# An eighth unit of hgrn's input weights kept in SBUF between two tiles, by way of an idle router place and a copy on ScalarE

## The chip, the cores and the metric

The kernel runs on one core of a Trainium2 chip, in one launch. The metric is the device time of the launch in microseconds. The kernel before takes 1483.97 us in the median of three runs (1483.34 to 1484.56).

## What is computed

A trunk of two layers over 256 positions of 1024 values, all in float32. Layer 0 mixes positions with windowed attention, layer 1 with HGRN2, a gated linear recurrence. After each comes PEER, a mixture of 16384 single-neuron experts. Cut to what matters:

```python
def hgrn2(xn, w_in, lower_bound, out_gain, w_out):
    q, f, i, g = split(xn @ w_in, 4)            # w_in is 1024 x 4096: 16 MiB
    ...                                          # gates, chunkwise recurrence
    return (rmsnorm(o, out_gain) * silu(g)) @ w_out

def block(xb):                                   # peer_ffn, 128 positions at a time
    q = xb @ w_q                                 # the router: 8 heads, 2 halves
    ...                                          # top 16 of 16384 for each head and position
    u = u_tab[expert]
    act = gelu(einsum('pd,phkd->phk', xb, u))
    return einsum('phk,phkd->pd', gates * act, v_tab[expert])

for i in range(2):
    h = h + (swa_attention, hgrn2)[i](rmsnorm(h, mixer_norm[i]), ...)
    h = h + peer_ffn(rmsnorm(h, ffn_norm[i]), ...)
```

## The kernel before, in words

The 256 positions are two tiles of 128, so the PEER blocks are four **phases** (layer 0 tile 0, layer 0 tile 1, layer 1 tile 0, layer 1 tile 1) of 128 **rows**. A row is one gather on POOL: for each of 128 positions the u and v rows of one expert, 8 KB, one MiB in all, into one of eight places of `ring`. DVE takes the dot product with xn (L1135), ScalarE Gelu, coefficient and a diagonal matrix of it (`diag`, L572), and PE adds the v rows into PSUM by that diagonal (L1545), or, for the rows of `VECTOR_ROWS`, DVE adds them into h (L1144). Gather n waits until the place of row n - 8 is free (`slots_free` from PE, `v_added` from DVE).

Beside the rows of phase p the engines do the mixer and the router for the other tile: attention in phase 0, hgrn for tile 0 in phase 1, hgrn for tile 1 in phase 2. Every engine has the same program: `foreground` of the row, then `beside(p, q)`, which says what belongs to row q. hgrn takes two heads at a time (four steps i of 20 rows, from row 8). Step i does `project` in 14 rows, levels of the chunk scan (`scores` on PE, `produce` and `extend` on DVE) in rows r = 16 to 24, the output in r = 26 (`h_o`), squares of it on ScalarE in r = 27, and the projection out in r = 33 to 36. The scan's scratch is in the first 2048 words of `mix` (hkq, sufpre, kq). The fourth step of phase 1 is done with it at row 94; phase 2 writes it next at row 22.

hgrn's input weights come in 32 **units** of one MiB, 16 for each tile; unit x is quarter x % 4 of the weights of step x // 4. Tile 1 takes the heads in the order 3, 2, 0, 1, so that it begins with the weights with which tile 0 ended. A unit lies in a **place**: 0 to 2 are in `wmix`, 3 and 4 in the room of router pair 3 (`wroute`), 5 and 6 in that of router pair 2. `UNIT_KEPT` says which units of tile 1 are still there from tile 0 (16 to 22), `UNIT_PLACE` where each lies, and `UNIT_LOADS` before which row SP's program has its load. SP's program is in order and has no clock of its own: what it issues is held by waits alone. A load into place 0 to 2 waits until the last unit there has been used (`h_proj`), one into a router place until the router has been used for phase 1 (`r_score`).

The four router pairs of layer 1 are loaded by `load_route` (L463 on): pair 0 in phase 1, pair 1 at row 104 of phase 1, which in order is right behind the third output load `load_hgrn_out` (row 85), pairs 3 and 2 in phase 2 when the kept units in their room have been used. PE asks for pair 1 at row 120 of phase 1, for the third unit of phase 2's router (`pair_projects`, `route_begin`).

Functions that the change and the prediction's steps touch: `unit_weights` (L382), `load_unit` (L444), `load_route` (L463), `copy` (L571, its operation L572), ScalarE's `beside` (L697), `project` (L1396) and the tables at L140.

Of the kernel before, what the change touches and what calls it, by code (L numbers as in the profile page):

```python
# [16 lines left out]
D = 1024  # L17
KT = D // P
EPS = 1e-6
HALF = 512  # L20
ITERS = 4
# [27 lines left out]
MIXED = 105  # L49
UNITS = 5  # L50
UNIT_HOMES = 3
UNIT_PLACES = 7
PAIR_ORDER = ((0, 1, 2, 3), (0, 1, 2, 3), (0, 1, 3, 2), (0, 1, 3, 2))
CHUNKS = 6
FIRST_CHUNK = (0, 2, 3, 4, 5)
HEAD_EXP = (115, 124)
RESIDUAL = 32


# [76 lines left out]
def unit_part(x):  # L136
    return x % 4 // 2, x % 2


UNIT_PLACE = (0, 1, 2, 0, 1, 2, 0, 1, 5, 6, 2, 0, 3, 4, 1, 0,  # L140
              3, 4, 1, 0, 5, 6, 2, 1, 0, 2, 1, 0, 2, 1, 0, 2)
UNIT_KEPT = {16: 12, 17: 13, 18: 14, 19: 15, 20: 8, 21: 9, 22: 10}
UNIT_LOADS = {0: {40: 0, 61: 1, 82: 2},
              1: {12: 3, 15: 4, 19: 5, 22: 6, 32: 7, 33: 8, 34: 9, 35: 10, 39: 11, 59: 12, 60: 13, 62: 14, 63: 15},
              2: {19: 23, 22: 24, 39: 25, 42: 26, 52: 27, 56: 28, 59: 29, 62: 30, 72: 31}}


def unit_load(x):
# [20 lines left out]
def trunk(nc, x, cos, sin, masks_attn, masks_hgrn, ident_in, place_in, gains, mixer_gain, sinks, lb_raw, out_gain,  # L169
          attn_in, attn_out, hgrn_in, hgrn_out, route_w, experts, out):  # L170
    with ExitStack() as ctx:
# [192 lines left out]
        h_decayed, h_decayedT_ps, h_decayedT = sem("h_decayed"), sem("h_decayedT_ps"), sem("h_decayedT")  # L364
        h_o, h_sq, h_ims, h_rstd = sem("h_o"), sem("h_sq"), sem("h_ims"), sem("h_rstd")
        h_on_ready, h_oT_ps, h_oT_ready = sem("h_on_ready"), sem("h_oT_ps"), sem("h_oT_ready")
        h_outproj = sem("h_outproj")
        r_proj, r_qT, r_score, r_top = sem("r_proj"), sem("r_qT"), sem("r_score"), sem("r_top")
        r_done, r_gate, g_shift, g_exp = sem("r_done"), sem("r_gate"), sem("g_shift"), sem("g_exp")

# [11 lines left out]
        def unit_weights(place):  # L382
            if place < UNIT_HOMES:
                return wmix[:, place]
            pair, at_ = ITERS - 1 - (place - UNIT_HOMES) // 2, (place - UNIT_HOMES) % 2
            return wroute[:, pair, at_ * 2 * D:(at_ + 1) * 2 * D]

# [54 lines left out]
        @block.sync  # L442
        def _(sp):
            def load_unit(x):  # L444
                place, (j, half) = UNIT_PLACE[x], unit_part(x)
                tile, i = x // 16, x // 4 % ITERS
                if x < UNIT_HOMES:
                    sp.wait_ge(a_outproj, ITERS + 1 + x)
                elif place < UNIT_HOMES:
                    sp.wait_ge(h_proj, last_use_of_place(x) + 1)  # L450
                else:
                    sp.wait_ge(r_score, CHUNKS + (6 if place < UNIT_HOMES + 2 else 5))
                sp.dma_start(unit_weights(place), hgrn_in[heads_at(tile, i) * 2 + j][:, half * 2 * D:(half + 1) * 2 * D]).then_inc(whgrn_in[place], 16)

            def load_hgrn_out(tile, i):
                n = tile * ITERS + i
                if n > 0:
                    sp.wait_ge(h_outproj, n)
                else:
                    sp.wait_ge(a_outproj, 2 * ITERS)  # L460
                sp.dma_start(bands(wmix[:, UNIT_HOMES], HH), hgrn_out[heads_at(tile, i)]).then_inc(whgrn_out_in, 16)

            def load_route(layer, pair):  # L463
                if layer and pair < 2:
                    sp.wait_ge(r_score, CHUNKS + 3 + pair)
                elif layer:
                    sp.wait_ge(h_proj, 18 if pair == 3 else 22)
                elif pair == ITERS - 1:
                    sp.wait_ge(a_outproj, ITERS)
                elif pair == 2:  # L470
                    sp.wait_ge(a_proj, 2 * ITERS)
                sp.dma_start(wroute[:, pair], route_w[layer * ITERS + pair]).then_inc(wroute_in[pair], 16)

            def hgrn_loads(p, q):
                tile = 1 - own_tile(p)
                for i in range(ITERS):
                    r = q - HEAD - HGRN_PERIOD * i
                    if r == 37 and i < ITERS - 1:
                        load_hgrn_out(tile, i + 1)

            sp.dma_start(h[:, 0], x[0]).then_inc(x0_in, 16)
            for to, of in ROPE:
                sp.dma_start(to, of).then_inc(rope_in, 16)
            half = AIN // 2
            sp.dma_start(win0(0)[:, 0:half], attn_in[0][:, 0:half]).then_inc(wattn0_in[0], 16)
            sp.dma_start(win0(0)[:, half:AIN], attn_in[0][:, half:AIN]).then_inc(wattn0_rest, 16)
            sp.wait_ge(x0_in, 16)
            sp.dma_start(win0(1), attn_in[1]).then_inc(wattn0_in[1], 16)
            sp.wait_ge(wattn0_rest, 16)
            sp.dma_start(win0(2), attn_in[2]).then_inc(wattn0_in[2], 16)  # L490
            sp.wait_ge(wattn0_in[1], 16)
            sp.dma_start(win0(3), attn_in[3]).then_inc(wattn0_in[3], 16)
            sp.dma_start(h[:, 1], x[1]).then_inc(x1_in, 16)
            sp.wait_ge(wattn0_in[2], 16)
            for g in range(ITERS):
                sp.dma_start(wout0(g), attn_out[g]).then_inc(wout0_in[g], 16)
            load_route(0, 0)
            sp.dma_start(gain_rows[:], gains).then_inc(gain_in, 16)
            for to, of in LATE:
                sp.dma_start(to, of).then_inc(late_in, 16)  # L500
            load_route(0, 1)
            load_route(0, 3)
            for p in range(PHASES):
                for q in range(PER):
                    if p == 0 and q == LAST_AHEAD[-1] + 1:
                        load_route(0, 2)
                    elif p == 1 and q == 4:
                        load_route(1, 0)
                    elif p == 1 and q == 104:
                        load_route(1, 1)  # L510
                    elif p == 2 and q == 15:
                        load_route(1, 3)
                    elif p == 2 and q == 36:
                        load_route(1, 2)
                    if q in UNIT_LOADS.get(p, {}):
                        load_unit(UNIT_LOADS[p][q])
                    if p == 0:
                        if q == 103:
                            load_hgrn_out(0, 0)
                    elif p < 3:  # L520
                        hgrn_loads(p, q)
                    if p == 3 and q == 5:
                        sp.wait_ge(norm_done, norm_at(3, 0) + 1)
                        sp.dma_start(out[0], xn[:, 0]).then_inc(out_done, 16)
            sp.wait_ge(norm_done, norm_at(3, 1) + 1)
            sp.dma_start(out[1][:, HALF:D], xn[:, 1, HALF:D]).then_inc(out_done, 16)
            sp.wait_ge(out_done, 16 * (TILES + 1))
# [40 lines left out]
        def _(act):  # L568
# [128 lines left out]
            def beside(p, q):  # L697
# [27 lines left out]
                for i in range(ITERS):  # L725
                    if p == 0:
                        attention(i, q - ATTN_HEAD - ATTN_PERIOD * i)
                    else:
                        hgrn(tile, i, q - HEAD - HGRN_PERIOD * i)
                if q == MIXED + 2:  # L730
                    act.wait_ge(h_ready, evacuations(p) + 1)
                    norm_squares(norm_at(p, 1), tile)
                elif q == MIXED + 5:
                    norm_sqrt(norm_at(p, 1), rroute[:, tile:tile + 1])
# [530 lines left out]
        def _(pe):  # L1265
# [130 lines left out]
            def project(n, r):  # L1396
# [6 lines left out]
                for u in range(2):  # L1403
                    x = 4 * n + r // 7 * 2 + u
                    load, half = unit_load(x), unit_part(x)[1]
                    place = UNIT_PLACE[x]
                    w = unit_weights(place).rearrange("p (k c) -> p k c", k=KT // 2)
                    for c in range(3):
                        for k in range(KT // 2):
                            step, cost = cost * 7 // 32, cost + 1 + c // 2  # L1410
                            if step != r % 7:
                                continue
                            if c == 0 and k == 0:
                                pe.wait_ge(whgrn_in[place], 16 * loads_into_place(load))
                            first, end, key = u == 0 and k == 0 and c == 0, u == 1 and k == KT // 2 - 1, half * KT // 2 + k
                            if c < 2:
                                last = nc.tensor.matmul(ab[:, j, c * P:(c + 1) * P], w[:, k, c * P:(c + 1) * P], xTs[:, 0, key],  # L1417
                                                        start=first, stop=end, skip_group_check=True)
                            else:
                                last = nc.tensor.matmul(ab[:, j, 2 * P:4 * P], xTs[:, 0, key], w[:, k, 2 * P:4 * P],  # L1420
                                                        start=first, stop=end, skip_group_check=True)
                                if k == KT // 2 - 1:
                                    last.then_inc(h_proj, 1)
# [312 lines left out]
```

## Time and profile before

| what | value |
|---|---|
| runs | 1483.34, 1483.97, 1484.56 us |
| the profiled execution | 1483.46 us |
| its span, first to last instruction | 1481.7 us |
| mean granted TensorE clock | 0.967 |
| moved by DMA | 603.44 MB |

The profile is of one execution. Busy times of engines lie beside each other, and their shares of the span are means over stages that have different limits. In a row of waits, "A <- B: x, n, m" says that A was idle for x us in n times, m at the longest, until B released it. In a timeline a bracket says how long the engine was idle before and what ended that. The prediction's rows stand below, after the change.

### The profile page before, as it was taken

The page shows a single profiled execution, that of the slowest core. Times are in us where ns is not written, and L with a number is a line of the kernel's source. Part 1 is how long each engine was busy: PE and PEld are TensorE (multiplying, and loading weights), DVE is VectorE, ACT ScalarE, POOL GpSimd, SP SyncE. Part 2 cuts the span into 40 slices and gives each one's busy share as a digit, 9 for nine tenths or more (in the row PEclk, how much of TensorE's full clock was granted, in tenths as well). Part 3 has the DMA queues.
Part 4 walks back from the last instruction along what each step waited for, and adds up shares of the span by engine and source line. Part 5 has one row for each costly group of instructions (what it writes and reads, how often), then busy time and mean ns, then how long its engine had stood idle before and what let it go on. Part 6 is the DMA issues. An engine that isn't in the chain of part 4 may idle for free.

```text
span 1481.7 us, 15275 instructions
## 1 busy us (share of the span) xinstructions
PE 1289.1 (87%) x4728; PEld 712.4 (48%) x4728; DVE 1075.9 (73%) x2659; ACT 612.0 (41%) x1826; POOL 603.0 (41%) x521
## 2 busy tenths in 40 slices
PE   8998987978888999798997799978999789877777
PEld 5664544434545657464454465745545344422222
DVE  3578887865787788796589778788759877675444
ACT  3344344343443343343455335234445443443334
POOL 0144455543444234333445434433444454434442
PEclk9999999999999999999999999999999899999999
DMA  9499999999999999999999999999999999999996
GB/s 371 178 403 421 421 420 422 421 421 421 422 420 421 411 419 402 421 422 422 421 420 421 422 398 401 421 422 420 413 421 421 415 421 421 421 421 421 422 422 268
DMA packets 83393, 603.44 MB, mean 407 GB/s; under 512 B 9904, under 2 KB 10608, under 8 KB 12016
## 3 DMA queue, kind: packets, MB, share of 16 engines
q0 software_dynamic: 74016, 536.90, 87.6%
q1 hardware_dynamic: 8576, 65.05, 10.7%
q8 instruction: 37, 0.61, 0.2%
q10 hardware_dynamic: 720, 0.52, 0.1%
q14 instruction: 44, 0.36, 0.1%
HBM read 601.39 MB, written 1.05 MB: 407 GB/s over the span
## 4 chain that ended last, share of the span: by engine, by line
DMA 45%; PE 32%; DVE 13%; ACT 8%; issue 2%; POOL 0%; DVEq 0%; POOLq 0%; ACTq 0%
DMA ring<-experts,idx 44%; PE acc L1545 19%; DVE ring L1135 7%; PE rbank L1495 3%; ACT diag L572 2%; PE ab L1417 1%; PE acc L1274 1%; ACT L683 1%; ACT coef L572 1%; PE ab L1420 1%; PE y L1285 1%; ACT gel L683 1%; DMA ring<-attn_in 1%; ACT L678 1%; DVE h L1144 1%
## 5 line engine op out<-in xcount | busy, mean ns | idle before, releaser
L1545 PE MATMUL acc<-ring,diag 128*128 128x512 f32 x1772 | 881.6, 625 | 175.2 <-ACT diag L572 163.7
L552 POOL DMA_INDIRECT ring<-experts,idx x510 | 596.7, 1170 | 801.1 <-PE acc L1545 672.3
L1135 DVE CUSTOM_DVE_ANT_0 ring<-ring,xn 128x1024 f32<-128x1024 f32 x512 | 624.3, 1221 | 279.3 <-DMA ring<-experts,idx 276.2
L1545 PEld LDWEIGHTS acc<-ring,diag 128*128 128x128 f32 x1772 | 317.9, 195 | 558.5 <-ACT diag L572 302.2
L683 ACT ACTIVATE gel<-dots 128x1 f32<-128x1 f32 x512 | 103.6, 202 | 746.0 <-DVE dots L1135 745.2
L572 ACT ACTIVATE diag<-ident,coef 128x128 f32<-128x128 f32 x443 | 178.0, 402 | 14.5
L572 ACT ACTIVATE coef<-gate,gel 128x1 f32<-128x1 f32 x512 | 150.9, 295 | 26.6 <-DVE h L1144 10.2
L1495 PEld LDWEIGHTS rbank<-xTs,wroute 128*128 128x128 f32 x832 | 113.3, 195 | 54.3 <-issue 53.3
L1495 PE MATMUL rbank<-xTs,wroute 128*128 128x128 f32 x832 | 114.7, 279 | 0.3 <-issue 0.3
L1144 DVE SCALAR_TENSOR_TENSOR h<-ring,coef,h 128x1024 f32<-128x1024 f32 x69 | 88.4, 1282 | 4.5 <-ACT coef L572 4.5
L1417 PEld LDWEIGHTS ab<-xTs,wmix 128*128 128x128 f32 x384 | 51.0, 195 | 12.8 <-issue 12.1
L1417 PE MATMUL ab<-xTs,wmix 128*128 128x128 f32 x384 | 52.3, 277 | 0.0
L1420 PE MATMUL ab<-wmix,xTs 128*128 128x256 f32 x192 | 51.0, 387 | 0.0
L683 ACT ACT_TABLE_LOAD x35 | 44.9, 1283 | 0.6
L1135 DVE DVE_READ_ACCUMULATOR2_ANT dots<- 128x1 f32 x512 | 42.1, 82 | 0.0
L1420 PEld LDWEIGHTS ab<-wmix,xTs 128*128 128x128 f32 x192 | 34.7, 195 | 10.8 <-issue 8.2
L1473 PE MATMUL y<-wmix,xn 128*128 128x512 f32 x64 | 32.7, 592 | 0.0
L678 ACT ACT_TABLE_LOAD x19 | 24.4, 1283 | 0.3
L1433 PEld LDWEIGHTS cbank<-mix 128*128 128x128 f32 x128 | 18.9, 196 | 10.1 <-issue 10.1
L1433 PEld LDWEIGHTS ab<-mix 128*128 128x128 f32 x128 | 18.4, 196 | 8.5 <-issue 8.0
L535 POOL MEMSET xn<- 128x256 f32 x1 | 0.3, 312 | 54.4 <-PE acc L1269 54.4
L915 DVE TENSOR_TENSOR mix<-mix 128x256 f32<-128x256 f32 x48 | 20.4, 425 | 1.7
(290 smaller groups left out, 1021.6 us busy)
## 6 DMA issues: line engine op xcount, KB each, us to landing
wmix<-hgrn_in SPq DMA_DIRECT2D x21, 1024.0 KB, 9.3
wroute<-route_w SPq DMA_DIRECT2D x8, 2304.0 KB, 13.0
ring<-experts,idx POOLq DMA_INDIRECT x510, 15.1
wmix<-hgrn_out SPq DMA_DIRECT2D x7, 1024.0 KB, 9.5
wmix<-attn_out SPq DMA_DIRECT2D x4, 1024.0 KB, 10.8
wroute<-hgrn_in SPq DMA_DIRECT2D x4, 1024.0 KB, 14.1
ring<-attn_in SPq DMA_DIRECT2D x2, 1536.0 KB, 9.1
ring<-attn_in SPq DMA_DIRECT2D x2, 768.0 KB, 8.1
```

What stands on the lines that cost most here:

```text
L552: pool.indirect_dma_start(out=ring[:, k * 2 * D:(k + 1) * 2 * D], out_offset=None, in_=experts, in_offset=bass.IndirectOffsetOnAxis(ap=idx ...
L572: return act.activation(to, of, ACT.Copy, scale=scale)
L678: act.activation(ge[:, hs], cvs[:, hs], ACT.Exp, scale=rroute[:, tile:tile + 1]).then_inc(g_exp, 1)
L683: link(act.activation(gel[:, k:k + 1], dots[:, k:k + 1], ACT.Gelu))
L1135: dve.tensor_tensor_reduce(out=u_rows(k), in0=u_rows(k), in1=xn[:, tile], scale=1.0, scalar=0.0, op0=ALU.mult, op1=ALU.add, accum_out=dots ...
L1144: dve.scalar_tensor_tensor(h[:, tile], v_rows(k), coef[:, c:c + 1], h[:, tile], ALU.mult, ALU.add).then_inc(v_added, 1)
L1417: last = nc.tensor.matmul(ab[:, j, c * P:(c + 1) * P], w[:, k, c * P:(c + 1) * P], xTs[:, 0, key], start=first, stop=end, skip_group_check ...
L1420: last = nc.tensor.matmul(ab[:, j, 2 * P:4 * P], xTs[:, 0, key], w[:, k, 2 * P:4 * P], start=first, stop=end, skip_group_check=True)
L1433: last = nc.tensor.matmul((cbank[:], ab[:, 1])[level % 2][:, own], keys, queries, start=True, stop=True)
L1473: last = nc.tensor.matmul(y[:, j * HALF:(j + 1) * HALF], h_oT(tile)[:, c], wmix[:, UNIT_HOMES, c * D + j * HALF:c * D + (j + 1) * HALF], s ...
L1495: last = nc.tensor.matmul(bank_of(u, c), weights_of(u)[:, (k * RHC + c) * P:(k * RHC + c + 1) * P], xTs[:, 1, k], start=k == 0, stop=k == ...
L1545: last = nc.tensor.matmul(acc[:, j * HALF:(j + 1) * HALF], diag[:, m % DIAGS], v_rows(k)[:, j * HALF:(j + 1) * HALF], start=n % PER == 0, ...
```

## The change

A unit place 7 is added in the room of router pair 1, which is idle from row 1 of phase 1 on. Unit 15 (the last of tile 0) is loaded there, and not into place 0. Place 0 therefore still holds unit 11 for tile 1's unit 23, whose load is left out; units 24 to 31 move on by one place. Unit 19 of tile 1 is the same quarter as unit 15, but by then the room is router pair 1's again: so in rows 96 to 99 of phase 1 ScalarE copies it, 512 of 2048 words at a time, into the scratch of `mix`, and PE's unit 19 reads it from there. Router pair 1's load waits for these copies.

```diff
-UNIT_PLACES = 7
+UNIT_PLACES = 8
+MOVED_UNIT, MOVED_PLACE = 15, 7
+MOVES, FIRST_MOVE = 4, 96
-UNIT_PLACE = (0, 1, 2, 0, 1, 2, 0, 1, 5, 6, 2, 0, 3, 4, 1, 0,
-              3, 4, 1, 0, 5, 6, 2, 1, 0, 2, 1, 0, 2, 1, 0, 2)
-UNIT_KEPT = {16: 12, 17: 13, 18: 14, 19: 15, 20: 8, 21: 9, 22: 10}
+UNIT_PLACE = (0, 1, 2, 0, 1, 2, 0, 1, 5, 6, 2, 0, 3, 4, 1, 7,
+              3, 4, 1, 7, 5, 6, 2, 0, 1, 2, 0, 1, 2, 0, 1, 2)
+UNIT_KEPT = {16: 12, 17: 13, 18: 14, 19: 15, 20: 8, 21: 9, 22: 10, 23: 11}
-              2: {19: 23, 22: 24, 39: 25, 42: 26, 52: 27, 56: 28, 59: 29, 62: 30, 72: 31}}
+              2: {22: 24, 39: 25, 42: 26, 52: 27, 56: 28, 59: 29, 62: 30, 72: 31}}
...
         def unit_weights(place):
+            if place == MOVED_PLACE:
+                return wroute[:, 1, 0:2 * D]
...
             def load_unit(x):
+                elif place == MOVED_PLACE:
+                    sp.wait_ge(r_score, CHUNKS + 4)
...
             def load_route(layer, pair):
-                if layer and pair < 2:
-                    sp.wait_ge(r_score, CHUNKS + 3 + pair)
+                if layer and pair == 0:
+                    sp.wait_ge(r_score, CHUNKS + 3)
+                elif layer and pair == 1:
+                    sp.wait_ge(unit_moved, MOVES)
...
+                if p == 1 and FIRST_MOVE <= q < FIRST_MOVE + MOVES:
+                    s = slice((q - FIRST_MOVE) * 2 * D // MOVES, (q - FIRST_MOVE + 1) * 2 * D // MOVES)
+                    if q == FIRST_MOVE:
+                        act.wait_ge(h_o, ITERS)
+                    copy(mix[:, s], unit_weights(MOVED_PLACE)[:, s]).then_inc(unit_moved, 1)
...
-                    w = unit_weights(place).rearrange("p (k c) -> p k c", k=KT // 2)
+                    w = (mix[:, 0:2 * D] if x == MOVED_UNIT + 4 else unit_weights(place)).rearrange("p (k c) -> p k c", k=KT // 2)
-                            if c == 0 and k == 0:
+                            if c == 0 and k == 0 and x == MOVED_UNIT + 4:
+                                pe.wait_ge(unit_moved, MOVES)
+                            elif c == 0 and k == 0:
                                 pe.wait_ge(whgrn_in[place], 16 * loads_into_place(load))
```

## Rows read from the trace of the kernel before

**Rows 1.** The page: span, busy time of the engines, bytes moved

```profile
span 1481.7 us, 15275 instructions
PE 1289.1 (87%) x4728; PEld 712.4 (48%) x4728; DVE 1075.9 (73%) x2659; ACT 612.0 (41%) x1826; POOL 603.0 (41%) x521
DMA packets 83393, 603.44 MB, mean 407 GB/s; under 512 B 9904, under 2 KB 10608, under 8 KB 12016
```

**Rows 2.** Waits of the whole span: us in total, times, longest

```profile
POOL ring L552 <- PE acc L1545: 672.3, 385, 8.4
DVE ring L1135 <- DMA ring<-experts,idx: 276.2, 235, 5.1
```

**Rows 3.** Windows: length, each engine's busy us, PE clock, DMA share, GB/s

```profile
600.00:830.00 230.00, 202.70 (x752) 115.55 (x751) 180.41 (x457) 103.49 (x296) 102.38 (x85) 0.96 1.01 421
857.50:912.50 55.00, 55.00 (x274) 38.08 (x273) 45.96 (x131) 20.00 (x62) 20.89 (x18) 0.99 0.98 392
880.00:912.50 32.50, 32.50 (x148) 21.85 (x148) 29.07 (x92) 12.85 (x39) 12.61 (x11) 1.00 0.95 373
```

**Rows 4.** SP's timeline: start, us, issue; several issues in one line are merged

```profile
596.84 10.44 SPq L453 DMA_DIRECT2D wmix<-hgrn_in  x2
...
676.47 0.45 SPq L472 DMA_DIRECT2D wroute<-route_w  x1
...
825.99 0.33 SPq L472 DMA_DIRECT2D wroute<-route_w  x1
835.71 17.39 SPq L453 DMA_DIRECT2D wmix<-hgrn_in  x2
...
896.98 0.33 SPq L472 DMA_DIRECT2D wroute<-route_w  x1
```

**Rows 5.** The page's DMA issues: KB each, us from issue to landing

```profile
wmix<-hgrn_in SPq DMA_DIRECT2D x21, 1024.0 KB, 9.3
wroute<-route_w SPq DMA_DIRECT2D x8, 2304.0 KB, 13.0
```

**Rows 6.** DVE's timeline: dot products that waited for their row

```profile
710.95 1.23 DVE L1135 CUSTOM_DVE_ANT_0 ring<-ring,xn 128x1024 f32<-128x1024 f32 x1 [0.96 <-DMA ring<-experts,idx]
...
862.54 1.22 DVE L1135 CUSTOM_DVE_ANT_0 ring<-ring,xn 128x1024 f32<-128x1024 f32 x1 [2.19 <-DMA ring<-experts,idx]
...
913.16 1.23 DVE L1135 CUSTOM_DVE_ANT_0 ring<-ring,xn 128x1024 f32<-128x1024 f32 x1 [1.34 <-DMA ring<-experts,idx]
```

**Rows 7.** PE's timeline: the rows' matmuls, with the gap before them

```profile
695.15 3.78 PE L1545 MATMUL acc<-ring,diag 128*128 128x512 f32 x4 [4.60 <-ACT diag L572]
...
717.02 1.98 PE L1545 MATMUL acc<-ring,diag 128*128 128x512 f32 x4 [1.81 <-ACT diag L572]
764.12 6.28 PE L1545 MATMUL acc<-ring,diag 128*128 128x512 f32 x14 [0.69 <-ACT diag L572]
...
854.87 5.32 PE L1545 MATMUL acc<-ring,diag 128*128 128x512 f32 x8 [2.13 <-ACT diag L572]
...
864.87 1.94 PE L1545 MATMUL acc<-ring,diag 128*128 128x512 f32 x4
...
868.43 1.88 PE L1545 MATMUL acc<-ring,diag 128*128 128x512 f32 x4
```

**Rows 8.** POOL's gathers (L552) issued from 880 to 896 us

```profile
DMA to landing us min/median/max: 8.1/9.9/13.3
```

**Rows 9.** POOL's gathers (L552) issued from 745 to 765 us

```profile
DMA to landing us min/median/max: 11.7/12.4/13.7
```

**Rows 10.** ScalarE's groups by shape: a copy of 128x512

```profile
L572 ACT ACTIVATE rqT<-rbank 128x512 f32<-128x512 f32 x12 | 7.0, 586 | 4.8 <-PE rbank L1495 4.8
```

**Rows 11.** Windows in phase 2, columns as in rows 3

```profile
1030.00:1040.00 10.00, 7.95 (x20) 4.26 (x21) 8.60 (x20) 4.98 (x14) 2.83 (x3) 0.83 1.01 422
1040.00:1050.00 10.00, 10.00 (x29) 4.71 (x28) 5.81 (x16) 4.71 (x14) 3.46 (x3) 1.00 1.00 406
1050.00:1060.00 10.00, 9.68 (x37) 5.37 (x35) 9.62 (x24) 3.59 (x12) 5.42 (x4) 1.00 1.01 403
```

More of the change, by code:

```diff
@@ L366, in trunk @@
         h_on_ready, h_oT_ps, h_oT_ready = sem("h_on_ready"), sem("h_oT_ps"), sem("h_oT_ready")
-        h_outproj = sem("h_outproj")
+        h_outproj, unit_moved = sem("h_outproj"), sem("unit_moved")
         r_proj, r_qT, r_score, r_top = sem("r_proj"), sem("r_qT"), sem("r_score"), sem("r_top")
```

## The prediction

> **What bounds the kernel now.** The page comes first: one core, span 1481.7 us, 603.44 MB moved at a mean of 407 GB/s [rows 1]. PE is busy for 87% and DVE for 73%, so neither limits over the whole span, and the transfers are the first suspect. The longest waits say the same from both ends: POOL, which issues the gathers, waits 672.3 us for PE to free a place of the ring, and DVE waits 276.2 us for gathered rows [rows 2]. A ring of eight places that is always full, with rows still late, means a queue in front of the DMA engines.
>
> A mean over stages hides who is last in each, so next come windows. From 600 to 830 us the DMA engines move 421 GB/s at a share of 1.01 [rows 3]; I take 421 as their ceiling here. At that rate one MiB (1.0486 MB, one gathered row or one unit) takes 2.49 us. From 857.5 to 912.5 us it is another picture: PE is busy 55.00 of 55.00 us and the DMA engines move only 392, and within that, from 880 to 912.5, 373 [rows 3]. There they run dry: 32.5 x (421 - 373) / 421 = 3.7 us of their time is unused. The kernel has two regimes, and the change's transfer has to be placed in one of them.
>
> SP's timeline places it. Router pair 3 is issued at 825.99 and two units follow, at 835.71 and 17.39 us later, so at 853.1 less the issue's own length [rows 4]. They are units 23 and 24: after the loads of routers 1 and 3 they are the next in phase 2's list. The next load, router pair 2, is at 896.98 [rows 4].
>
> **The change part by part.**
> Load of unit 23, removed. Unit 24 now goes to place 1 and waits for the end of unit 18, which is what unit 23 waited for. So a unit is still issued at 835.71; the one missing is that at 853.1. Units 25 to 31 keep their waits (ends of 22 to 28) under new places. Gross value: 1.0486 MB at 421 GB/s = -2.49 us of DMA time, in flight from 853 to about 862 (a unit lands 9.3 us after its issue [rows 5]).
>
> Who is last at 853 to 862? DVE waits 2.19 us for a gathered row at 862.54 [rows 6]; that wait is the missing unit's, and it will go. But PE had its last gap, 2.13 us, before 854.87 [rows 7], and from there on it is never free. Its four matmuls of one row start at 864.87 and those of the next at 868.43, 3.56 us later, where the DMA engines deliver a row each 2.49 us [rows 7]. PE is slower than the transfers here, since hgrn's level matmuls and the router's projections (L1433, L1495) stand between the rows. An earlier row waits for PE instead of DVE waiting for the row. POOL gets its places from PE, so the gathers of this stretch are issued when they are now; the DMA engines only reach the hole at 880 with 2.49 us less queued. The hole grows from 3.7 to 6.2 us. When DVE next waits for a row, 1.34 us at 913.16 [rows 6], that row's gather was issued after the hole and after router pair 2 at 896.98, neither of which moved. Given back: +2.49 us. Net 0. Bounds: -2.49 (all kept) and 0.
>
> The trace-analysis page of the Trainium skill ("Perfetto Trace Analysis", section Identifying the Most-Contended Engine) says to optimize the engine with the highest occupancy or utilization first, and adds that kernels can have several regimes. Read over the whole span its first half names the DMA engines and gives -2.49; the row at 857.5 sets PE as last, and gives 0. I go by the row.
>
> Unit 15, moved. It waited for unit 11's end in place 0, 10.44 us after unit 14's issue at 596.84, less one issue's length; its new place is free long before, so it is issued right behind unit 14, some 10 us sooner [rows 4]. From 600 to 830 the DMA engines are full [rows 3]: the same bytes in another order. Cost 0; its cover is that queue. Bounds 0 to +0.3 (rows later by up to 2.49 us around 605 to 615, after which rows are waited for anyway).
>
> Four copies on ScalarE. 128x512 each; a ScalarE copy of this shape takes 0.586 us out of PSUM [rows 10]; out of SBUF I take 0.6. Four are 2.4 us in rows 96 to 99 of phase 1. Their wait, the fourth output of hgrn, has already been taken by the Square at row 95, so it adds nothing. Behind each copy stands the next row's Gelu; row 97 (the 226th dot product of L1135) starts at 710.95 after DVE waited 0.96 us for the row [rows 6], so there ScalarE has time to spare. Cost 0; without that cover 2.4, the upper bound.
>
> PE takes unit 19 from the scratch instead of place 0. The instructions are the same; its wait (copies done at about 713) is met more than 100 us before the first use in phase 2. Unit 23 reads unit 11 in place 0, loaded in phase 1. Both 0.
>
> Router pair 1 (2304 KB, 5.6 us of DMA time) moves. It was issued at 676.47 behind the third output load; now SP waits for the fourth copy. The rows no longer delayed come up to 5.6 us sooner: row 99 at about 711, copies done and load issued at about 713. It lands 13.0 us later [rows 5], so at 726; PE asks for it at row 120, some 20 rows x 2.49 = 50 us behind the issue. Behind this wait on SP stands only router pair 3 at 825.99 [rows 4]. What is late next: without the burst at 676, POOL keeps less queued from 680 to 700, in the same part of a head (its last levels, DVE-heavy) in which phase 2, at 1040 to 1060, has a hole: 406 and 403 GB/s, so 10 x (15 + 18) / 421 = 0.8 us [rows 11]. Bounds 0 to +0.8; I take +0.3, nearer to 0: phase 2's hole comes right after ten us with PE's clock granted at 0.83 [rows 11], a delay of its own that phase 1 need not have.
>
> Sum: -2.49 + 2.49 + 0 + 0 + 0.3 = +0.3. The profiled execution took 1483.46 us (span 1481.7 and 1.8 around it), so 1483.8; the runs' median 1483.97 is 0.5 above it, so I predict 1484.3.
>
> **The rivals.**
> A, the whole transfer is gained: PE only looks full and could start rows sooner. For it: ends of matmuls are modelled, and DVE's 2.19 us wait is real. Against it: the 3.56 us from row to row, and the hole. 1483.97 - 2.49 = 1481.5, or 1481.8 with the 0.3.
> B, more than the transfer: without router pair 1 at 676, PE's gap of 4.60 us before 695.15 goes, behind which four matmuls ran 3.78 us where 1.88 is usual, at the lower of TensorE's two clock levels (1.2 GHz) [rows 7]. It adds 1.9 us of PE time, useful only if PE is last there; the full DMA window [rows 3] speaks against it. 1481.5 - 1.9 = 1479.6.
> C, slower: the router's burst now stands at 713 to 726, right before PE's densest tail. In the kernel before, PE's last gap was 1.81 us ahead of 717.02 and none follows until 764.12 [rows 7]. A gap like that at 695.15 now comes there, and the rows behind it cost 1.9 us more of PE. The cushion: a gather takes at least 11.7 us to land in this tail [rows 9] and 8.1 where the DMA engines ran dry [rows 8], so 3.6 us of queue. C decides once PE is later by more than the queue covers; with one slow group passed on in full it costs 1.9 + 0.8 = +2.7, so 1486.7, with two +4.6, so 1488.6.
> The Trainium skill's "TensorE: Matmul & The Clock Gate" (part 1) says that the throttled clock is the default and activity releases it. The row at 695.15 agrees; that is why the change's later burst can hurt at all.
> That nothing is saved at all because unit 23 is still loaded is excluded: it has no slot in the list.
>
> **How the numbers follow.** A measurement of this kernel can tell about 0.2% (3.0 us) from no change: faster is under 1481.0, slower over 1486.9. Forecast (1483.7 to 1484.8): 0.62. A: 0.20, of which 0.02 falls under 1481.0. B: 0.07, all faster. C: 0.11, of which 0.06 is slower. Faster 0.09, slower 0.06, same 0.85. The range takes in A with 0.2 us of scatter and C to the price of one slow group less the 0.5 that the queue takes: 1481.3 to 1486.2; outside are B and a part of A below (0.09), and most of C above (0.08).
>
> **What would show it.** 602.39 MB instead of 603.44; 19 unit loads into wmix and 5 into wroute where there were 21 and 4. The wait of 2.19 us near 862 is gone, PE has no gap from about 855 to 912 and the rows' spacing there is unchanged; 880 to 912.5 moves some 32 GB/s less (2.49 of 32.5 us). Pair 1 is issued near 713. Wrong if 857 to 912 shortens by 2 us, if PE shows gaps in it, or if the stretch 713 to 770 shows gaps of DMA or a lower clock.

## The result, and the profile after

The changed kernel takes 1481.58 us (median of 19 runs, 1479.80 to 1482.96), the kernel before 1483.78 us in as many runs beside it. The ratio is 0.9983, with a 95% interval of 0.9976 to 0.9989. So it is faster, by 2.2 us of the medians (2.5 by the ratio), which is all of one transfer's 2.49 us or nearly so. That is less than the 3.0 us that the prediction asked of "faster", but the interval leaves no change out. The forecast had +0.3; the time lies inside the range given, at its lower end, and is what rival A said. The profiled execution took 1480.87 us, its span 1479.1.

First the page of the changed kernel, which answers to [rows 1, 5]:

```profile
span 1479.1 us, 15278 instructions
PE 1286.4 (87%) x4728; PEld 709.4 (48%) x4728; DVE 1075.6 (73%) x2659; ACT 614.0 (42%) x1830; POOL 600.7 (41%) x521
DMA packets 83249, 602.39 MB, mean 407 GB/s; under 512 B 9888, under 2 KB 10592, under 8 KB 12000
...
wmix<-hgrn_in SPq DMA_DIRECT2D x19, 1024.0 KB, 9.5
wroute<-route_w SPq DMA_DIRECT2D x8, 2304.0 KB, 12.2
...
wroute<-hgrn_in SPq DMA_DIRECT2D x5, 1024.0 KB, 14.7
```

The bytes are those foretold, 1.05 MB fewer, and so are the loads by tile. SP's timeline [rows 4] has unit 15's load right behind unit 14's, router pair 1 behind the copies, one unit at 835.73 and none at 853:

```profile
597.07 0.48 SPq L459 DMA_DIRECT2D wmix<-hgrn_in  x1
597.60 0.49 SPq L459 DMA_DIRECT2D wroute<-hgrn_in  x1
...
713.98 112.37 SPq L480 DMA_DIRECT2D wroute<-route_w  x2
835.73 0.33 SPq L459 DMA_DIRECT2D wmix<-hgrn_in  x1
896.51 0.33 SPq L480 DMA_DIRECT2D wroute<-route_w  x1
```

Next the dot products on DVE's timeline [rows 6]:

```profile
860.26 1.22 DVE L1148 CUSTOM_DVE_ANT_0 ring<-ring,xn 128x1024 f32<-128x1024 f32 x1
...
911.17 1.22 DVE L1148 CUSTOM_DVE_ANT_0 ring<-ring,xn 128x1024 f32<-128x1024 f32 x1
914.34 1.23 DVE L1148 CUSTOM_DVE_ANT_0 ring<-ring,xn 128x1024 f32<-128x1024 f32 x1 [0.30 <-DMA ring<-experts,idx]
```

Read them beside [rows 6]. The wait of 2.19 us near 862 is gone. The row whose dot product started at 913.16 starts at 911.17, 2.0 us sooner. From here on a row is named by its phase and its number in it: this one is 2.42, row 42 of phase 2. Set side by side, the starts of all 512 rows say when the time is won: rows 1.112 and 2.0 to 2.24 stand within 0.4 us of before; 2.32 to 2.40 are 0.5 us sooner; 2.42 is 2.0, 2.48 is 2.1, 2.56 is 2.5 sooner, and from there the difference is 2.3 to 2.7 in all but 14 rows, which show more; row 3.116 starts at 1446.3 before and at 1443.7 after. So 0.5 us is won where PE becomes dense, nothing more while it is, and the rest, 2.0 us, right behind the dip in the DMA rate.

The windows of that stretch [rows 3]:

```profile
857.50:912.50 55.00, 54.70 (x274) 38.17 (x275) 47.17 (x134) 20.05 (x63) 21.16 (x19) 1.00 0.97 387
880.00:912.50 32.50, 32.50 (x146) 21.71 (x146) 29.78 (x94) 12.91 (x40) 12.76 (x12) 1.00 0.93 366
```

and PE's timeline [rows 7], whose spacing of rows is the old one (864.46 to 867.97 is 3.5 us), with PE still without a gap from 858 on:

```profile
854.86 1.98 PE L1560 MATMUL acc<-ring,diag 128*128 128x512 f32 x4 [2.11 <-ACT diag L580]
857.80 1.98 PE L1560 MATMUL acc<-ring,diag 128*128 128x512 f32 x4 [0.95 <-ACT diag L580]
...
864.46 1.88 PE L1560 MATMUL acc<-ring,diag 128*128 128x512 f32 x4
...
867.97 1.88 PE L1560 MATMUL acc<-ring,diag 128*128 128x512 f32 x4
```

PE sets this stretch until 905, as foretold. But the rate from 880 to 912.5 fell by 7 GB/s, not by 32: 32.5 x 7 / 421 = 0.5 us more is unused, where 2.5 were to be given back. The gathers issued from 888.5 to 896 us show the other side of it. In the kernel before, from issue to landing:

```profile
DMA to landing us min/median/max: 8.1/8.3/13.3
```

In the changed kernel:

```profile
DMA to landing us min/median/max: 6.1/6.3/7.2
```

A transfer that lands in 8.1 us where another lands in 6.1 did not meet an empty queue. That is where the explanation starts.

A gather's semaphore is raised 16 times, and the trace has the moment of each. I take each as the share of one of the 16 DMA engines; the page of the Trainium skill that says so is named near the end. The table (worked out from these events; us) gives for a row its gather's issue, the median of its 16 shares and the last of them:

```
        before                      after
row     issue   median  last        issue   median  last
2.24    835.1   852.1   858.5       835.2   852.8   857.5
2.25    843.5   854.6   862.5       843.5   855.3   860.0
2.28    852.4   864.6   870.0       852.4   862.8   867.5
2.32    864.2   874.5   879.9       863.8   872.7   877.4
2.36    878.3   884.5   889.9       877.8   883.0   887.3
2.38    885.9   891.2   895.8       885.4   890.7   893.4
2.39    890.1   895.3   898.3       889.6   894.8   895.8
2.40    892.7   897.9   900.8       892.2   897.4   898.3
2.41    895.5   900.8   908.8       895.0   900.2   902.2
2.42    898.9   908.7   913.1       898.5   908.2   909.7
2.44    903.6   916.2   920.0       903.1   915.6   916.8
```

Take row 2.40 before. Its shares came 5.0 5.1 5.1 5.2 5.2 5.2 5.2 5.2 5.2 5.2 5.2 5.3 5.4 5.4 5.5 and 8.1 us behind the issue. Fifteen engines had nothing else to do, and one was 2.6 us behind them. In the hole its last shares still came a row's time apart or more (882.4, 884.8, 887.3, 889.9, 893.3, 895.8, 898.3, 900.8 for rows 2.33 to 2.40), so the engine behind them never ran dry (taking it to be the same one throughout, as the even spacing has it; the events do not name it). A row is usable with its sixteenth share: the dot product that waits for row 2.25 starts at 862.54, its last share lands at 862.5, and for row 2.42 these are 913.16 and 913.1. The last column is 2.4 to 2.6 us sooner in every row from 2.25 to 2.40 (3.3 in 2.37). The median column is 1.8 us sooner at 2.28 and only 0.5 at 2.38 to 2.40, the 0.5 of the issue: fifteen engines did give back in the hole what they had won, and nobody was waiting for them.

### The profile page after: what moved, and what is told of

The parts are those of the page before. It is cut to its first block, busy times and chain, and to the rows that moved or that the text cites. A ratio compares the mean times of both kernels' runs of the same rounds, so it can differ in the third digit from the quotient of the medians.

```text
span 1479.1 us, 15278 instructions
## 1 busy us (share of the span) xinstructions
PE 1286.4 (87%) x4728; PEld 709.4 (48%) x4728; DVE 1075.6 (73%) x2659; ACT 614.0 (42%) x1830; POOL 600.7 (41%) x521
## 3 DMA queue, kind: packets, MB, share of 16 engines
HBM read 600.34 MB, written 1.05 MB: 407 GB/s over the span
## 4 chain that ended last, share of the span: by engine, by line
DMA 47%; PE 32%; DVE 11%; ACT 8%; issue 2%; POOL 0%; DVEq 0%; POOLq 0%; ACTq 0%
DMA ring<-experts,idx 46%; PE acc L1560 18%; DVE ring L1148 6%; PE rbank L1510 2%; PE ab L1432 2%; ACT diag L580 2%; ACT L691 1%; PE acc L1287 1%; ACT coef L580 1%; PE ab L1435 1%; PE y L1298 1%; ACT L686 1%; ACT gel L691 1%; DMA ring<-attn_in 1%; DVE h L1157 1%
## 5 line engine op out<-in xcount | busy, mean ns | idle before, releaser
L1432 PEld LDWEIGHTS ab<-xTs,wmix 128*128 128x128 f32 x352 | 45.6, 192 | 10.6 <-issue 10.0
L1432 PE MATMUL ab<-xTs,wmix 128*128 128x128 f32 x352 | 47.2, 275 | 0.0
L1435 PE MATMUL ab<-wmix,xTs 128*128 128x256 f32 x176 | 46.5, 385 | 0.0
L1435 PEld LDWEIGHTS ab<-wmix,xTs 128*128 128x128 f32 x176 | 31.7, 195 | 9.6 <-issue 7.3
```

## The experiments

Two theories stood at first. **S**: the slowest of the 16 engines counts, it has work all through the hole, and so a transfer less is worth its 2.49 us. **M**: the forecast is right on the hole, and what was won comes from the parts moved in phase 1. In the edits, a + line replaces the - line.

**The unit is loaded again (e1).** The changed kernel with every move and copy kept, but unit 23 loaded as before:

```diff
-              3, 4, 1, 7, 5, 6, 2, 0, 1, 2, 0, 1, 2, 0, 1, 2)
-UNIT_KEPT = {16: 12, 17: 13, 18: 14, 19: 15, 20: 8, 21: 9, 22: 10, 23: 11}
+              3, 4, 1, 7, 5, 6, 2, 1, 0, 2, 1, 0, 2, 1, 0, 2)
+UNIT_KEPT = {16: 12, 17: 13, 18: 14, 19: 15, 20: 8, 21: 9, 22: 10}
...
-              2: {22: 24, 39: 25, 42: 26, 52: 27, 56: 28, 59: 29, 62: 30, 72: 31}}
+              2: {19: 23, 22: 24, 39: 25, 42: 26, 52: 27, 56: 28, 59: 29, 62: 30, 72: 31}}
...
-                    sp.wait_ge(h_proj, last_use_of_place(x) + 1)
+                    sp.wait_ge(h_proj, 20 if x == 24 else last_use_of_place(x) + 1)
```

> The changed kernel with the load of unit 23 put back, at its old time; the earlier load of unit 15, the copies and the later router load stay. Theory S (the slowest DMA engine): in the kernel before, one of the 16 DMA engines finishes its share of each gather 2.6 to 5 us after the other fifteen, and in the hole at 880 to 900 us only those fifteen run empty; so the removed transfer's share on the slow engine is worth its whole 2.49 us. S expects the time of the kernel before, 1483.8 within 0.5. Rival M (the prediction's: the hole swallows the transfer, and the 2.2 us come from what moved in phase 1) expects 1481.6 as the changed kernel.

Measured: 1483.91 us, 0.9997 of the kernel before (0.9988 to 1.0006). Its gathers issued from 891 to 898 land as before:

```profile
DMA to landing us min/median/max: 8.2/8.4/13.4
```

So the gain is the transfer. The moves and the four copies together are worth -1.8 to +0.9 us by that interval, and M's -2.2 lies outside it: M is out.

**The unit alone, left out (e2).** The kernel before, nothing moved; PE multiplies with unit 14's weights, still in place 1, where it should with unit 23's, and the load of unit 23 is left out. The transfer that is missing here is the one at 835.7, and not the one at 853.

```diff
-UNIT_KEPT = {16: 12, 17: 13, 18: 14, 19: 15, 20: 8, 21: 9, 22: 10}
+UNIT_KEPT = {16: 12, 17: 13, 18: 14, 19: 15, 20: 8, 21: 9, 22: 10, 23: 14}
...
-              2: {19: 23, 22: 24, 39: 25, 42: 26, 52: 27, 56: 28, 59: 29, 62: 30, 72: 31}}
+              2: {22: 24, 39: 25, 42: 26, 52: 27, 56: 28, 59: 29, 62: 30, 72: 31}}
```

> The kernel before without the load of unit 23, nothing else changed: PE multiplies with unit 18's weights, still in place 1, in the place of unit 23's. The missing transfer is now the one at 835.7 us, unit 24 stays at 853. S expects 1483.8 - 2.5 = 1481.3. M expects 1483.8, no gain. That the moves in phase 1 cost something is tested beside it: under S this kernel minus the changed one is their price, -0.3 to 0.

Measured: 1482.21 us, 0.9986 (0.9977 to 0.9995): -1.8 by the medians, -2.1 by the ratio. The size is near that of the change, but it is not won in the same place. Row 2.22 in the kernel before and in this one:

```profile
852.59 1.23 DVE L1135 CUSTOM_DVE_ANT_0 ring<-ring,xn 128x1024 f32<-128x1024 f32 x1 [1.26 <-DMA ring<-experts,idx]
```

```profile
850.66 1.23 DVE L1135 CUSTOM_DVE_ANT_0 ring<-ring,xn 128x1024 f32<-128x1024 f32 x1 [1.26 <-DMA ring<-experts,idx]
```

This execution was 0.6 us behind at row 2.16, so 2.5 us are won by row 2.22, ahead of PE's dense stretch, and the queue in the hole is not shorter: row 2.40 lands 9.1 us behind its issue (8.1 before). So e2 says what a transfer is worth where rows are waited for, as e4 below, and it is no test of S. Neither run says why the hole took nothing back in the changed kernel.

**One transfer more, issued inside the hole (e3).** The kernel before, and unit 24 loaded a second time, at 889.23 in the trace (cut to what matters):

```diff
+                    if p == 2 and q == 30:
+                        sp.wait_ge(whgrn_in[0], 16 * loads_into_place(24))
+                        sp.wait_ge(h_proj, 21)
+                        sp.dma_start(unit_weights(0)[0:128], hgrn_in[heads_at(1, 2) * 2][0:128, 0:2 * D]).then_inc(extra_in, 16)
...
+                                if x == 24:
+                                    pe.wait_ge(extra_in, 16)
```

> The kernel before with a second load of unit 24 (1 MiB, 128 partitions, same place) issued when h_proj reaches 21, some 885 us, in the hole of the mean rate. S expects the slow engine to pay for its share in full: 1483.8 + 2.5 = 1486.3. M expects the hole (3.7 us of unused mean rate) to take it for nothing: 1483.8 to 1484.3.

Measured: 1486.10 us, 1.0012 (1.0003 to 1.0021): +1.8 by the ratio, +2.1 by the medians, for 2.49 us of transfer put just where the mean rate had 3.7 us to spare. SP's timeline has the issue:

```profile
889.23 0.33 SPq L520 DMA_DIRECT2D wmix<-hgrn_in  x1
```

The window of the hole in this kernel:

```profile
880.00:912.50 32.50, 31.94 (x158) 22.26 (x156) 26.18 (x85) 12.62 (x38) 12.99 (x12) 1.00 0.97 390
```

And on DVE's timeline the dot product of row 2.40:

```profile
910.43 1.23 DVE L1139 CUSTOM_DVE_ANT_0 ring<-ring,xn 128x1024 f32<-128x1024 f32 x1 [2.09 <-DMA ring<-experts,idx]
```

The hole did take the bytes (390 GB/s where [rows 3] have 373). The time was not free: the load's own shares landed at 895.2 to 895.8 on fifteen engines and at 898.7 on the sixteenth, and row 2.40's at 6.3 to 7.6 us and 16.0 us behind its issue. The median share of that row comes 1.6 us later than in the kernel before (6.8 against 5.2), the last one 7.9 us.

**A second transfer left out (e4).** The changed kernel, unit 24 not loaded either (the load at 835.73; PE takes unit 14's weights in its place):

```diff
-UNIT_KEPT = {16: 12, 17: 13, 18: 14, 19: 15, 20: 8, 21: 9, 22: 10, 23: 11}
+UNIT_KEPT = {16: 12, 17: 13, 18: 14, 19: 15, 20: 8, 21: 9, 22: 10, 23: 11, 24: 14}
...
-              2: {22: 24, 39: 25, 42: 26, 52: 27, 56: 28, 59: 29, 62: 30, 72: 31}}
+              2: {39: 25, 42: 26, 52: 27, 56: 28, 59: 29, 62: 30, 72: 31}}
```

> The changed kernel with the load of unit 24 left out as well (PE multiplies with unit 18's weights in its place). In the changed kernel the slowest engine's share of rows 39 and 40 lands 6.3 and 6.1 us after the issue, where an empty engine takes 5.4: 0.7 to 0.9 us of queue are left. S expects that much more and no more: 1481.6 - 0.8 = 1480.8, with the sixteen shares of those rows landing together. A plain count of bytes expects 1481.6 - 2.5 = 1479.1. M expects 1481.6.

Measured: 1479.48 us, 0.9965 (0.9951 to 0.9978), 2.1 below the changed kernel by the medians, 2.7 by the ratios. The 0.8 expected of S is wrong, and the plain count of bytes (1479.1) is met. I had put this load into the hole's stretch, and it stands ahead of it: from 826 to 857 both PE and DVE wait for rows. The window of the kernel before:

```profile
826.00:857.00 31.00, 19.47 (x67) 11.85 (x68) 20.61 (x34) 11.46 (x32) 11.53 (x9) 0.85 1.01 422
```

The same window of this kernel:

```profile
826.00:857.00 31.00, 21.06 (x76) 12.99 (x75) 22.78 (x40) 12.18 (x34) 13.85 (x11) 0.89 1.01 422
```

PE is busy 19.47 of 31.00 us there. Rows come sooner at once, PE's dense stretch begins sooner as a block, and the queue in the hole is what it was (rows 2.37 to 2.40 land 7.5, 8.0, 6.3 and 6.1 us behind their issue, those of the changed kernel 7.5, 7.9, 6.3 and 6.1). To test how much a saving in PE's own stretch is worth, the bytes must go inside it. The next four do that.

**Two half gathers in PE's stretch (e7, e8).** Rows 2.29 and 2.30 gather only their u half, 0.5 MiB less each, and add v rows left from eight rows earlier; once on the changed kernel, once on the kernel before:

```diff
+                if n in (2 * PER + 29, 2 * PER + 30):
+                    pool.indirect_dma_start(
+                        out=u_rows(k), out_offset=None, in_=half_experts,
+                        in_offset=bass.IndirectOffsetOnAxis(ap=idx[:, q:q + 1], axis=0),
+                    ).then_inc(slot_in[k], 16)
```

> The changed kernel with rows 29 and 30 of phase 2 gathering only the u half (their v rows stay those of eight rows earlier, so two rows of the output's sum are wrong): 1 MiB less, in flight near 865 us, inside the stretch that PE sets. This is the limit of theory S. In the changed kernel the slowest engine has 0.7 to 0.9 us of queue left at rows 39 and 40, so S expects 0.8 of the 2.49 us: 1481.6 - 0.8 = 1480.8, and all sixteen shares of rows 38 to 40 within 5.6 us. A plain count of bytes expects 1479.1.

> The same two half gathers in the kernel before. There the slowest engine has 2.7 us of queue at row 40 (8.1 against 5.4), so S expects nearly all of the 2.49 us: 1483.9 - 2.4 = 1481.5, as the changed kernel, though no load and nothing of phase 1 was touched. M (the hole of the mean rate swallows it) expects 1483.9.

Measured: on the kernel before 1481.63 us, 0.9986 (0.9977 to 0.9996), so these 2.49 us of DMA time are worth 2.0 to 2.1; on the changed kernel 1480.71 us, 0.9979 (0.9969 to 0.9989) of before, where the changed kernel itself has 0.9983 (0.9976 to 0.9989): 0.6 us by the ratios, 0.7 by the medians, each against the kernel before beside it, with intervals that overlap for the most part. The same bytes are worth a transfer in one kernel and little or nothing in the other.

**Four half gathers (e9, e10, e11).** Rows 2.28 to 2.31, so 2 MiB or 4.98 us of DMA time; on the changed kernel, on the kernel before, and with them the changed kernel unaltered:

```diff
-                if n in (2 * PER + 29, 2 * PER + 30):
+                if 2 * PER + 28 <= n < 2 * PER + 32:
```

> The changed kernel with rows 28 to 31 of phase 2 gathering only the u half (four rows of the output's sum get stale v rows): 2 MiB less in the stretch that PE sets, 4.98 us of DMA time. If the queue of the slowest engine is all that can be saved there (0.7 to 0.9 us), this is the changed kernel less 0.8: 1480.8, and no better than two half gathers. A plain count of bytes expects 1481.6 - 5.0 = 1476.6.

> The same four half gathers in the kernel before. The queue of the slowest engine at row 40 is 2.7 us (8.1 against 5.4 for an empty one), so S expects 1483.8 - 2.7 = 1481.1 and no more; the count of bytes 1478.8; the prediction's hole of the mean rate 1483.8.

> The changed kernel itself, beside the two on the same chip: 1481.6, and e9 0.8 us below it by S, 5 us below it by the count of bytes.

Measured beside each other: the changed kernel 1481.04 us, 0.9980 (0.9970 to 0.9989); with four half gathers 1481.12 us, 0.9980 (0.9971 to 0.9989). Two MiB less there are worth nothing that can be measured: the means of the eleven runs of each differ by 0.2 us, and the runs of one kernel scatter over 3.5 us or more. That rules out the 4.98 of the count of bytes, but does not tell the 0.8 of S from 0. In the traces not even that is won: row 2.40 lands 0.6 us sooner behind its issue, but rows 2.41 and 2.42, issued about when router pair 2 is, land after 7.1 and 11.5 us (7.2 and 11.6 in the changed kernel beside it, e11). On the kernel before the four half gathers give 1481.33 us, 0.9985 (0.9976 to 0.9994): 2.2 by the ratio, 2.9 by the medians, of 4.98. That is a limit, and its size is that of the slow engine's queue: row 2.40 lands 8.1 us behind its issue before, 6.1 in the changed kernel, and 5.5 (e10) and 5.6 us (e9) in these two, where nothing is left queued. 8.1 - 5.4 = 2.7 us could be won before, and at most 6.1 - 5.4 = 0.7 are left after. The windows have meanwhile come to the same rate. The kernel before with four half gathers (e10):

```profile
880.00:912.50 32.50, 32.50 (x147) 21.73 (x147) 29.75 (x93) 12.86 (x39) 12.60 (x12) 1.00 0.92 358
```

The changed kernel with them (e9):

```profile
880.00:912.50 32.50, 32.50 (x146) 21.74 (x145) 29.82 (x93) 13.35 (x41) 13.24 (x12) 1.00 0.92 361
```

**Which engine lags (e5, e6).** Two tries to move the extra work off an engine. The first is the extra load of the hole in 120 partitions instead of 128 (`[0:120]` in place of `[0:128]`). It went out in 15 shares:

> The kernel before with the extra load of e3 cut to 120 partitions. The Trainium skill's DMA: Bandwidth & Descriptors (Queues, rings and completion order) says that such a transfer goes to 15 engines, the lowest-numbered, and not to 16. If the slow engine is the last one, it is spared, and S expects the hole of the other fifteen to take the load: 1483.9 to 1484.3. If it is one of the fifteen: 1486.1, as e3. M expects 1484 in either case, but M has already failed in e3.

Measured: 1491.67 us, 1.0046 (1.0032 to 1.0060). Neither expected value was met; by the medians it is 5.6 us worse than the same load in 128 partitions (5.0 by the ratios), with fewer bytes. The rule that the expectation takes from the Trainium skill stands in that page's section Why a DMA increments its semaphore by 16 and not by 1. The trace of e5 keeps only a part of the load's shares, but that of e6 below agrees: there two loads of 120 and 8 partitions together raise their semaphore 25 times, as at 183.8 us, twice within 1 us of the issue and 23 times (15 and 8) from 11.7 to 14.1 us behind it. The window from 890 to 900 of this kernel:

```profile
890.00:900.00 10.00, 10.00 (x45) 6.45 (x44) 9.66 (x37) 3.32 (x13) 2.81 (x3) 1.00 0.99 289
```

The same window with the load in 128 partitions (e3):

```profile
890.00:900.00 10.00, 10.00 (x42) 6.37 (x41) 9.66 (x36) 3.77 (x15) 2.81 (x3) 1.00 0.98 380
```

The engines are as busy (0.99) and move a quarter less. The time says nothing on the lagging engine, since the form of the load costs more than what it was to show. The shares say something: row 2.37's last lands at 899.5 and row 2.38's at 903.5, 6.2 and 7.7 us later than in the kernel before (2.3 of them from earlier in this execution), while all other recorded shares of these rows land by 890.7 and 894.2; and of the load's own shares that the trace keeps, one comes at 902.31 and the others by 899.2. So the lagging engine had a share of this load and was not the one spared. The second try is the changed kernel with all its 24 unit loads in two parts:

```diff
-                sp.dma_start(unit_weights(place), hgrn_in[heads_at(tile, i) * 2 + j][:, half * 2 * D:(half + 1) * 2 * D]).then_inc(whgrn_in[place], 16)
+                for s in (slice(0, 120), slice(120, P)):
+                    sp.dma_start(unit_weights(place)[s], hgrn_in[heads_at(tile, i) * 2 + j][s, half * 2 * D:(half + 1) * 2 * D]).then_inc(whgrn_in[place], 16)
```

> The changed kernel with each of hgrn's 24 unit loads issued as two, of 120 and of 8 partitions. If the slow engine is the last one, it is spared in both, 24 times 2.49 us of its time; the others then carry more, and set the pace as soon as its lag (3 to 5 us) is gone. S then expects 3 to 15 us less than the changed kernel: 1467 to 1479. If the slow engine is one of the first eight, it gets 9 partitions' share in place of 8, 24 x 0.3 = 7 us more: 1489; if one of the next seven: 1481.6.

Measured: 1592.06 us, 1.0726 (1.0712 to 1.0741), for the changed kernel's bytes:

```profile
DMA packets 83418, 602.40 MB, mean 379 GB/s; under 512 B 10056, under 2 KB 10760, under 8 KB 12168
```

That is 110.5 us more than the changed kernel, 4.6 us for each of 24 loads, on top of some 2.5, and far above every value expected. Which of the fifteen engines lags stays open.

## Why the prediction was wrong

**Where it was right.** The load that goes is the one at 853, and the other keeps its 835.7. The wait of 2.19 us at 862 goes. PE sets the stretch from 858 to 905, its rows stay 3.5 us apart, and until 905 only 0.5 us is won. The bytes and the counts of loads are exact.

**The step that failed is the giving back of +2.49.** It took the mean rate of 373 GB/s from 880 to 912.5 for an empty queue ("There they run dry") and, in rival C, the shortest landing of 8.1 us for that of a dry engine. The rate is a sum over 16 engines, and 15/16 of it can fall while one engine is never idle. The floor is 5.0 to 5.5 us, seen in fifteen shares of row 2.40 and, once the bytes are gone, in all of them or nearly so (5.4 to 5.7 for the last shares of rows 2.37 to 2.40 in e10). The 8.1 us held a queue of 2.7 us on one engine, more than the 2.49 that were taken away. So the hole was wide for fifteen engines and closed for the sixteenth. In place of +2.49 the runs show nearly nothing given back: the sum is -2.49 plus what the slow engine gives back. That part is bounded by 0 and 0.3: its last shares are 2.5 us sooner up to row 2.40, and the ratio's -2.5 and the medians' -2.2 leave no more. The load put back (e1, 0 to the kernel before), the load added in the hole (e3, +1.8 to +2.1) and the bytes taken out of the stretch by other means (e8, -2.0 to -2.1) say the same.

**And what the row at 913.16 hangs on.** "That row's gather was issued after the hole and after router pair 2, neither of which moved": both stand (897.0 and 896.5). But row 2.41 ahead of it, issued at 895.5 and thus before pair 2's 2304 KB, was caught by them. On the slow engine it could get its turn only behind row 2.40 at 900.8, by which time the pair's share stood beside it: 13.3 us, last share at 908.8. With 2.5 us less in that one queue it landed at 902.2, 7.2 us behind its issue. [Rows 8] had this 13.3 beside 8.1 and 9.9, and the working used only the smallest. That the turn is shared in this way is my reading of the times; the times are the table's.

**The smaller terms.** Unit 15 sooner: 0 expected, and e1 has it with the copies and router pair 1 in its -0.03% +/- 0.09%. The four copies:

```profile
L580 ACT ACTIVATE mix<-wroute 128x512 f32<-128x512 f32 x4 | 2.5, 614 | 0.0
```

614 ns each where 0.6 us was taken from [rows 10], and hidden. Router pair 1 moved: +0.3 expected, which that interval (up to +0.9 us) cannot tell from 0; in the traces it is 0.1: row 2.0 starts at 788.9 in one kernel and 789.0 in the other. The windows in phase 2 that set this term, 406 and 403 GB/s [rows 11], are 422 and 423 here, so what was seen there was not a standing property of a head's last levels:

```profile
1040.00:1050.00 10.00, 10.00 (x33) 5.14 (x32) 8.40 (x19) 2.94 (x11) 5.01 (x4) 1.00 1.01 422
1050.00:1060.00 10.00, 9.40 (x32) 4.93 (x31) 9.59 (x23) 3.36 (x11) 3.91 (x4) 1.00 1.02 423
```

**The rivals.** A is the outcome, but not by its mechanism: up to 905 PE was full and could start nothing sooner than the 0.5 us. The forecast's weighing of A asked only whether PE was full, and the question that decided was whether the queue was empty. C's mechanism did occur, in the place named. The router's burst opened a gap and a slow group, at the granted clock of 0.89 from 720 to 730:

```profile
712.11 1.98 PE L1560 MATMUL acc<-ring,diag 128*128 128x512 f32 x4 [2.33 <-ACT diag L580]
728.26 3.47 PE L1560 MATMUL acc<-ring,diag 128*128 128x512 f32 x4 [4.49 <-ACT diag L580]
764.47 5.85 PE L1560 MATMUL acc<-ring,diag 128*128 128x512 f32 x13 [0.19 <-ACT diag L580]
```

It cost 0.1 us at most: the cushion, sized from the same floor, was 6.3 us (11.7 less 5.4) and not the 3.6 it was given, against one slow group's 1.9. That this is why is argued, not tested.

**What a page would have said.** The Trainium skill's "DMA: Bandwidth & Descriptors", section Latency and other measured facts, has two of the 16 DMA engines usually slower than the rest in traces, and as a best guess puts it down to how transfers described by GpSimd are fetched. The trace agrees in that a gather's stragglers are one or two (row 2.41 before: fourteen shares by 5.4 us, then 7.9 and 13.3); it does not say which engines they are, and no run here bears on the guess. The section Why a DMA increments its semaphore by 16 and not by 1 has each engine raise the semaphore by one once its own data has landed, and only the full count mean that all has. The trace agrees with its 16 events for a gather and the dot products that start with the last. The most-contended rule of the Trainium skill's "Perfetto Trace Analysis", set aside in the prediction in favour of the row at 857.5, gave the better figure here (-2.49), though by e9 it does not hold for a second transfer inside that stretch.

## What to carry to other kernels

Before you call a dip in the DMA rate idle time, look at the last share to land: compare the shortest landing in the dip with that of a truly empty queue (5.4 us for this 1 MiB gather), because a dip in the mean can hide one engine that never stops. Where compute sets a stretch, a transfer removed ahead of its dip is worth at most its own time or the slowest engine's queue above that floor, whichever is less (2.0 to 2.9 us measured where that is 2.5 or 2.7); where rows are waited for, it is worth about its own time (1.8 to 2.7 in e2 and e4). The next one of the kind inside the stretch has at most what is left of that queue: 0.7 us here, of which the runs show 0.0 to 0.7.

## What the runs showed of the hardware that was not expected

- **One share of each gather lands some 2.9 to 5.4 us behind the median of its sixteen** in rows 2.28 to 2.40 of the kernel before (row 2.28: median 864.6, last 870.0), and 3.8 to 6.6 us in phase 3. It differs a little between runs (4.7 in the changed kernel at row 2.28, 5.0 in another run of it) and changes at times in steps of about 0.97 us. Three such steps in phase 3, at 1213.1, 1278.8 and 1344.3 us, stand 2 to 2.7 us behind packets of 8 KB in an instruction queue (1211.1, 1276.1, 1342.2; each took 0.33 us). Four other 8 KB packets in that queue between 1202 and 1402 us (1202.8, 1245.6, 1321.3, 1401.4; 0.31 us each) are followed by none. That would fit one engine that also fetches part of the instructions; no run tested it.
- **A load of 120 partitions is slow out of proportion.** It went out in 15 shares, its 8 KB packets took 0.61 us in the median and 0.78 at most (0.31 and 0.33 in 128 partitions), and a part of the gathers' packets beside it slowed with it. Split in 120 and 8, each unit costs 4.6 us more, by e6. Why is not settled.
